# Telling the other engines that TensorE is done: a drain of its pipe, or the counters of finished products

## The chip, the cores and the metric

The kernel runs on one core of one Trainium2 chip. The metric is the device time of one execution in microseconds (us), as a median over runs. The core has five engines, each with an instruction queue of its own: TensorE (PE in the profile, its weight loads PEld), VectorE (DVE), ScalarE (ACT), GpSimd (POOL) and SyncE (SP), which here issues almost all transfers. Engines wait for each other on semaphores, counters that an instruction raises when it is done.

## The reference

One transformer block for 512 tokens of width 1024, then a second one with routed experts, all in float32.

```python
h = rms_norm(x, norm_pre[i])
(aq, ak, av, az, dq, dk, dv, db, da, dz, gate_att, gate_dn) = split_cols(h @ w_in[i])
...
o_att = gqa_attention(q, k, v).transpose(0, 2, 1, 3).reshape(B, S, ATT_W)
y_att = (o_att * jax.nn.silu(az)) @ w_br_att[i]
qkv = jax.nn.silu(short_conv(jnp.concatenate([dq, dk, dv], axis=-1), conv_w[i]))
...
o_dn = bidir_gated_deltanet(qd, kd, vd, g, beta).astype(x.dtype)
y_dn = (rms_norm(o_dn...) * jax.nn.silu(dz)) @ w_br_dn[i]
mix = (jax.nn.sigmoid(gate_att) * y_att + jax.nn.sigmoid(gate_dn) * y_dn) @ w_out[i]
x = x + rms_norm(mix, norm_post[i])
x = x + rms_norm(jax.nn.sigmoid(x @ w_ple_gate[i]) * (p[i] @ w_ple_proj[i]), ple_norm[i])
```

The second block modulates a normed x by columns computed from a condition vector (`w_ada_2`), mixes tokens by a gated linear attention in both directions and by pooling with four windows, projects with `w_out_2`, and then sends each token through two of 32 experts.

## The kernel before

The whole program is written out by hand, one instruction stream for each engine, with explicit semaphores. TensorE's stream sets the order of the work:

- Projections of the first block. Weights come in blocks of 1 MB (128 partitions, 8 chunks, 256 columns) in a fixed order, `weight_order`, into four slots, later two, then four again. SyncE's `stream_to` issues the load of block n into a slot as soon as the block that was in that slot before (`before[n]`) is used. `slot(key)` on TensorE waits for the load.
- Most projections are done two blocks at a time by `seven(u, ...)`, a scheme with seven half products instead of eight; there are 21 of these (u = 0 to 20), each some 112 matmuls of 256 columns. VectorE, ScalarE and GpSimd prepare sums of weights (`part_ready`, GpSimd line 2337) and of inputs (`term_ready`), and add up the results. The other projections are `feature_tile` and `token_tile`.
- `ada_rows` multiplies the condition by two blocks of `w_ada_2`. It is called 12 times, spread over the attention and the delta rule.
- Every product goes into one of eight PSUM banks, four of a ring called v (read by VectorE) and four of a ring called s (read by ScalarE mostly). `bank(r)` on TensorE takes the next bank of ring r and waits on `free_v` or `free_s`, and the last matmul of a product raises `full_v` or `full_s`. `jobs[r]` counts the products of a ring.
- Stage by stage the memory is used again for other things. At the end of stages 1 to 6 every engine raises `phase` by one, and whoever writes to the memory of the next stage waits until four engines have.

The stages in time, read from the lines of the instructions: projections for attention to 112 us, condition rows and turning q and k to 150, attention with gates to 262, four `seven` to 362 (stage 1 ends there), 24 tiles of the short convolution with the inverses prepared by VectorE to 571 (stage 2), eight steps of the delta rule to 689 (stage 3), output side of the first block and the start of the second to 986 (stage 4), projections, decay and pooling of the second to 1124 (stage 5), linear attention to 1176, `w_out_2` to 1250 (stage 6), routing, and from about 1284 to the end the experts, whose weights are streamed.

Three helpers of TensorE's stream and four single places tell the others that TensorE has read something for the last time. All do it by a drain: an instruction that waits until everything before it has left the array, and then raises a semaphore. `used` raises `w_used` once for each weight block, `leave_stage` and `phase` raise `phase`. The single places are one that raises `phase` at line 1460 (stage 4), one for each of four pooling products (line 1494, `pool_used`), one after the linear attention (line 1581, `gla_used`) and one at line 1638 (stage 6). One more stands in the loop over the experts (`wout_used`). In all there are 86 drains at line 1042, 4 at line 1045, and 4, 1, 1 and 1 at the single places: 97 ahead of the experts.

Of the kernel before, what the change touches and what calls it, by code (L numbers as in the profile page):

```python
# [14 lines left out]
P = 128  # L15
# [248 lines left out]
def build(nc, a, out, dumps):  # L264
    ctx = ExitStack()
    with ctx:
# [289 lines left out]
        def scratch(name, *shape):  # L556
# [11 lines left out]
        names = """chain_v chain_s chain_p phase full_v free_v full_s free_s w_used ld_const ld_vecs ld_rope  # L568
# [7 lines left out]
            lexp_ready ld_out half_win win_used wout_used ld_gs yb_ready hidT_ready sil_ready hid_ready out_ready picked_ready icol_ready rows_saved gla_used first_ready  # L576
            table_ready index_ready xg_k0 xg_k1 xe_ready st_y0 st_y1
            turns_ready sil_used pool_used zeroed dbp_ready mask_turned mask_kept last_ready""".split()
# [231 lines left out]

        block = ctx.enter_context(nc.Block())

        @block.sync
        def _(sp):
            issued = [0]

            def load(dst, src, name):
                sp.dma_start(dst, src).then_inc(s[name], 16)

            def stream_to(key):  # L820

                while True:
                    n = issued[0]
                    k, src, _, _ = weights[n]
                    if before[n] >= 0:
                        sp.wait_ge(s["w_used"], before[n] + 1)
                    sp.dma_start(slot_view(n), src).then_inc(s["ld_w", slot_of[n]], 16)
                    issued[0] += 1
                    if k == key:
                        return  # L830

            def load_win(n, x, part=0, parts=1):
                k = n % RING
                c = slice(part * KC // parts, (part + 1) * KC // parts)
                sp.dma_start(win[2 * k + x][:, c, :], win_src[n, x][:, c, :]).then_inc(s["ld_win", k], 16)

            def load_win_halves(n):
                k = n % RING
                for h, signal in ((0, s["half_win"]), (1, s["ld_win", k])):
                    c = slice(h * KC // 2, (h + 1) * KC // 2)  # L840
                    for x in range(2):
                        sp.dma_start(win[2 * k + x][:, c, :], win_src[n, x][:, c, :]).then_inc(signal, 16)

            def load_wout(n, x):
                k = n % RING
                sp.dma_start(wout[2 * k + x], wout_src[n, x]).then_inc(s["ld_wout", k], 16)

            def load_wout_early(x, c):
                sp.dma_start(wout_early[x, c], wout_src[RING, x][:, c, :]).then_inc(s["ld_pm", 0], 16)

            def save(t):
                sp.wait_ge(s["x3_ready"], t + 1)
                sp.dma_start(xn_dram[t * P:(t + 1) * P, :], x3n[:, t, :]).then_inc(s["ld_tile", t], 16)
                sp.dma_start(x3_dram[t * P:(t + 1) * P, :], x3[:, t, :]).then_inc(s["ld_tile", t], 16)

            def third_pair(t):
                sp.wait_ge(s["ld_tile", t], 48)
                sp.wait_ge(s["half_ready"], 2 * NT + NTC + t + 1)
                for x in range(2):
                    load_win(2, x, t, NT)  # L860

            for k in range(4):
                sp.dma_start(xr[:, 2 * k:2 * k + 2, :], a["x_t"][:, 2 * k:2 * k + 2, :]).then_inc(s["ld_tile", k], 16)
            stream_to(("qkv", 1))
            sp.wait_ge(s["ld_const"], 16)
            load(const[:, C_HEAD:], a["c_masks"][:, C_HEAD:], "ld_const")
            load(rope, a["c_rope"], "ld_rope")
            load(qkn[:, 0, :], a["q_norm"].partition_broadcast(P), "ld_rope")
            load(qkn[:, 1, :], a["k_norm"].partition_broadcast(P), "ld_rope")
            load(gpar[:, 0, :], a["a_log"].rearrange("a d h -> a (d h)").partition_broadcast(P), "ld_res")  # L870
            load(gpar[:, 1, :], a["dt_bias"].rearrange("a d h -> a (d h)").partition_broadcast(P), "ld_res")
            stream_to(("qkv", 3))
            sp.wait_ge(s["zeroed"], 2)
            load(y_dram[0:2 * SEQ, :].rearrange("(p r) (h n) -> p (r h) n", p=P, h=2),
                 arow.rearrange("p a n -> p (a n)").unsqueeze(1).broadcast_to([P, 16, 2 * WC]), "rows_saved")
            stream_to(("dz", 1))

            sp.wait_ge(s["phase"], 4 * 3)
            stream_to(("gd", 1))
            for t in range(NTC):  # L880
                load(ctxt[:, t, :], a["ctx_2"][0, t * P:(t + 1) * P, :], "ld_ctx")
            load(mixT.rearrange("p c n -> p (c n)"), mix_dram.rearrange("(p n) -> p n", p=P), "mix_kept")
            load(rowv, a["norm_post"].partition_broadcast(P), "ld_res")
            load(rowv2, a["ple_norm"].partition_broadcast(P), "ld_res")
            stream_to(("gd", 3))
            load(pinT, a["p_t"], "ld_p")
            stream_to(("brd", 3))
            for t in range(NT):
                load(x1[:, t, :], a["x"][0, t * P:(t + 1) * P, :], "ld_res")
            load(wa2, a["w_a2"].rearrange("p (c n) -> p c n", n=32), "ld_p")  # L890
            stream_to(("vp2", 1))

            sp.wait_ge(s["phase"], 4 * 4)
            load(bdec, a["b_decay_2"].rearrange("a d k -> a (d k)").partition_broadcast(P), "ld_small")
            sp.dma_start(gs_dram[0, :].rearrange("(c p) -> p c", p=P), gain[:, 16:24],
                         allow_slow_non_contiguous=True).then_inc(s["ld_gs"], 16)
            sp.dma_start(gs_dram[1, :].rearrange("(c p) -> p c", p=P), mod[:, 24:32, 0],
                         allow_slow_non_contiguous=True).then_inc(s["ld_gs"], 16)
            load(wpool, a["w_pool_2"][0].rearrange("g c d -> c g d"), "ld_small")
            for g in range(2):  # L900
                sp.dma_start(pm[:, g, :, :], a["c_pool"][:, g, :, :]).then_inc(s["ld_pm", g], 16)
            sp.wait_ge(s["zeroed"], 3)
            for q in range(4):
                for d in range(2):
                    load(wdec[32 * q + RANK * d:32 * q + RANK * (d + 1), d * 256:(d + 1) * 256],
                         a["w_decay_2"][0, d], "ld_small")
            stream_to(("qp2", 1))
            for g in range(2, 4):

                sp.wait_ge(s["pool_used"], g - 1)  # L910
                sp.dma_start(pm[:, g % 2, :, :], a["c_pool"][:, g, :, :]).then_inc(s["ld_pm", g % 2], 16)
            stream_to(("wo2", 1))
            sp.wait_ge(s["ld_gs"], 32)
            load(gsp[:, :, :], gs_dram.rearrange("a (p c) -> p a c", p=P), "ld_gs")
            load(wrt[:, :, 0:4], a["w_router_group_2"][0].rearrange("(c p) n -> p c n", p=P), "ld_wrt")
            load(wrt[:, :, 4:36], a["w_router_expert_2"][0].rearrange("(c p) n -> p c n", p=P), "ld_wrt")
            sp.wait_ge(s["kst_ready"], NT + NTC)
            load(wo23[0], wo23_src[0], "ld_small")

            sp.wait_ge(s["sprev_ready"], 1)  # L920
            load(wo23[1], wo23_src[1], "ld_small")

            sp.wait_ge(s["gla_used"], 1)
            for x in range(2):
                load_win(0, x)
            load_wout(2, 0)
            for t in range(NT - 1):
                save(t)
                third_pair(t)

            sp.wait_ge(s["w_used"], len(weights))
            load_win(1, 0)
            sp.wait_ge(s["phase"], 4 * 6)
            for x in range(2):
                load_wout(0, x)
            save(NT - 1)
            load(xn_dram[SEQ:, :].rearrange("o (p n) -> (o p) n", p=KC), zero[0:KC, :], "rows_saved")
            load_win(1, 1)
            for x in range(2):
                load_wout(1, x)  # L940

            sp.wait_ge(s["lg_ready"], 1)
            for k in range(2):
                sp.wait_ge(s[f"xg_k{k}"], 16)
            third_pair(NT - 1)
            for k in range(2):
                sp.wait_ge(s[f"st_y{k}"], 16)
            for x, c in wout_early:
                load_wout_early(x, c)
# [6 lines left out]
            with sp.Fori(0, rounds) as r:  # L956
# [25 lines left out]
                with sp.If(r + 1 < rounds):  # L982
                    for x, c in wout_early:
                        load_wout_early(x, c)
# [2347 lines left out]
```

## Time and profile before

| | |
|---|---|
| device time, median of 3 runs | 1535.87 us (1535.25 to 1537.34) |
| span of the profiled execution, first to last instruction | 1531.2 us |
| what lies around the span, against the median | 4.7 us |
| TensorE busy (matmuls) | 1414.3 us, 92% |
| VectorE / GpSimd / ScalarE busy | 721.2 / 420.5 / 383.3 us |
| moved by DMA | 236.51 MB |

The profiled execution's own time is not listed beside its span, so the span and the 4.7 us around it, taken against the median, stand for it. A matmul's end in the profile is modelled. Starts are recorded, so distances from start to start are what to read. "issue" as the reason of idle time means that the profile shows no wait that was fulfilled just then. Drains don't count as busy, but they can be looked up by their line.

### The profile page before, as it was taken

Reading aid. Unit: us, or ns where it says so; the run is one execution under the profiler, and the core shown is the slowest. Engines: PE = TensorE matmul, PEld = TensorE weight load, DVE = VectorE, ACT = ScalarE, POOL = GpSimd, SP = SyncE. Lnnn points to the kernel's source line nnn. Section 1 sums busy time; section 2 is a strip of 40 time slices with the busy share of each in tenths; the row PEclk is TensorE's granted clock in tenths of the full one; section 3 lists DMA queues with packets and bytes.
Section 4 is the critical chain, followed back from the end, with each engine's and each line's share of the span. In section 5 each row is a group of like instructions: output and inputs, shape, how many; then the busy total and the mean of one; then the engine's idle time right before and its main releaser. Section 6 shows DMA issues by size and latency. Waiting matters only on the chain. (4 is left out here: it accounts for less than half of the span.)

```text
span 1531.2 us, 22283 instructions
## 1 busy us (share of the span) xinstructions
PE 1414.3 (92%) x8580; PEld 959.5 (63%) x8580; DVE 721.2 (47%) x1280; ACT 383.3 (25%) x777; POOL 420.5 (27%) x316
## 2 busy tenths in 40 slices
PE   7998998999999999999999999999988979987886
PEld 5864444886454447877888868878757864332322
DVE  5251435223438987778624252731364454432325
ACT  2223445202343234332110032511251011000002
POOL 3420002630003617563555435044000003111110
PEclk9999999999999999999999999999999989999999
DMA  7227110122111212414332311241033379999996
GB/s 309 86 107 270 63 57 27 55 83 110 56 56 55 83 56 112 158 68 159 130 129 94 138 55 56 64 119 56 9 134 121 132 276 355 415 419 420 422 417 246
DMA packets 48151, 236.51 MB, mean 154 GB/s; under 512 B 12103, under 2 KB 13391, under 8 KB 27056
## 3 DMA queue, kind: packets, MB, share of 16 engines
q1 hardware_dynamic: 42432, 224.48, 37.8%
q0 software_dynamic: 5040, 8.27, 1.5%
q10 hardware_dynamic: 576, 2.36, 0.4%
q8 instruction: 69, 1.13, 0.3%
q14 instruction: 34, 0.28, 0.1%
HBM read 223.66 MB, written 21.51 MB: 160 GB/s over the span
## 5 line engine op out<-in xcount | busy, mean ns | idle before, releaser
L1092 PE MATMUL psv<-arena 128*128 128x256 f32 x1648 | 361.8, 380 | 2.9 <-issue 2.9
L1092 PEld LDWEIGHTS psv<-arena 128*128 128x128 f32 x1648 | 312.7, 190 | 47.7 <-issue 6.0
L2554 DVE TENSOR_TENSOR arena<-arena,psv 128x512 f32<-128x512 f32 (+1 forms) x99 | 68.6, 693 | 299.4 <-PE psv L1092 297.3
L1054 PE MATMUL psv<-arena,wslot 128*128 128x512 f32 x384 | 170.8, 598 | 0.5 <-issue 0.5
L1688 PE MATMUL pss<-arena 128*64 128x512 f32 x432 | 125.4, 641 | 15.8 <-DMA arena<-w_expert_in 14.6
L1054 PEld LDWEIGHTS psv<-arena,wslot 128*128 128x128 f32 x384 | 71.2, 190 | 84.0 <-issue 83.7
L1827 ACT ACTIVATE arena<-pss 128x512 f32<-128x512 f32 (+2 forms) x125 | 72.1, 577 | 152.7 <-PE pss L1054 73.5
L1054 PE MATMUL pss<-arena 128*128 128x512 f32 (+1 forms) x224 | 92.7, 566 | 6.8 <-ACTq L232 4.6
L2774 DVE SCALAR_TENSOR_TENSOR arena<-psv,ccols,arena 128x510 f32<-128x510 f32 (+1 forms) x96 | 71.9, 749 | 52.9 <-ACT arena L2007 49.6
L1092 PE MATMUL psv<-arena,wslot 128*128 128x256 f32 x384 | 86.9, 381 | 3.9 <-issue 1.9
L1688 PEld LDWEIGHTS pss<-arena 128*64 128x64 f32 x432 | 38.9, 147 | 70.4 <-issue 70.3
L1092 PEld LDWEIGHTS psv<-arena,wslot 128*128 128x128 f32 x384 | 72.4, 190 | 16.0 <-issue 5.4
L2337 POOL TENSOR_TENSOR arena<-wslot 128x1024 f32<-128x1024 f32 x11 | 25.8, 2349 | 205.6 <-PE pss L1225 114.8
L1092 PE MATMUL psv<-wslot,arena 128*128 128x256 f32 x320 | 76.8, 397 | 5.8 <-ACT arena L1886 3.5
L1092 PEld LDWEIGHTS psv<-wslot,arena 128*128 128x128 f32 x320 | 63.1, 199 | 17.3 <-ACT arena L1886 4.7
L1054 PEld LDWEIGHTS pss<-arena 128*128 128x128 f32 x224 | 41.5, 190 | 49.8 <-issue 40.7
L3236 DVE TENSOR_TENSOR arena<-pss,arena 128x256 f32<-128x256 f32 x16 | 6.8, 424 | 138.6 <-ACTq L232 138.6
L2355 POOL TENSOR_TENSOR arena<-arena 128x1024 f32<-128x1024 f32 x20 | 49.1, 2454 | 81.7 <-DVE arena L2647 36.4
L2551 DVE TENSOR_TENSOR arena<-arena 128x512 f32<-128x512 f32 (+2 forms) x64 | 51.7, 807 | 22.2 <-ACT arena L1963 11.3
L1707 PE MATMUL psv<-arena 128*64 128x512 f32 x248 | 58.5, 598 | 3.5 <-ACTq L232 2.0
L2681 DVE TENSOR_REDUCE small<-pss 128x1 f32<-128x512 f32 x32 | 22.1, 692 | 81.8 <-PE pss L1225 81.1
L2224 ACT ACTIVATE arena<-pss 128x256 f32<-128x256 f32 x16 | 6.1, 383 | 193.4 <-PE pss L1688 193.4
(397 smaller groups left out, 2079.0 us busy)
## 6 DMA issues: line engine op xcount, KB each, us to landing
wslot<-w_blocks SPq DMA_DIRECT2D x56, 1024.0 KB, 5.2
arena<-w_blocks SPq DMA_DIRECT2D x31, 1024.0 KB, 6.9
arena<-w_expert_out SPq DMA_DIRECT2D x31, 1024.0 KB, 25.4
arena<-w_expert_in SPq DMA_DIRECT2D x28, 1024.0 KB, 27.2
arena<-w_expert_in SPq DMA_DIRECT2D x28, 512.0 KB, 13.1
arena<-w_expert_in SPq DMA_DIRECT2D x6, 2048.0 KB, 19.8
y_dram<-arow SPq DMA_DIRECT2D x1, 4096.0 KB
arena<-c_pool SPq DMA_DIRECT2D x4, 1024.0 KB, 9.2
```

Source lines behind the costliest of these rows:

```text
L1054: m = mm(o, l, r, start=(n == 0), stop=(n == len(pairs) - 1))
L1092: m = mm(o[:, j * HALF_T:(j + 1) * HALF_T], l[:, c, j * P:(j + 1) * P], r[:, c, :], start=new and j == 0 and c == 0, stop=j == 1 and c == ...
L1688: m = mm(o[x * CAP:(x + 1) * CAP, :], xe[:, k, c, x * CAP:(x + 1) * CAP], win[2 * w + x][:, c, :], start=(c == 0), stop=(c == KC - 1))
L1707: m = mm(o[x * CAP:(x + 1) * CAP, :], hidT[:, k, c, x * CAP:(x + 1) * CAP], wout_home(n, x, c)[:, c0:c0 + 512], start=(c == 0), stop=(c == 1))
L1827: L.did(A(dst, src, func, **kw), s[sig] if sig else None, [s["free_s"]])
L2337: L.did(TT(part[0], a21, a22, ALU.add), s["part_ready"])
L2355: L.did(TT(term[n], lo, hi, ALU.subtract), s["term_ready"])
L2551: L.did(V.tensor_tensor(o, x, y, ALU.mult), *sig)
L2554: L.did(V.tensor_tensor(o, x, y, ALU.add), *sig)
L2681: L.did(V.tensor_reduce(c, pss[:, score_job[i] % 4, :], AXX, ALU.max))
L2774: L.did(V.scalar_tensor_tensor(o[:, lo:hi], b[:, lo + m:hi + m], tap(j, k), o[:, lo:hi], ALU.mult, ALU.add), s["conv_ready"] if k == 4 els ...
L3236: L.did(V.tensor_tensor(hid[:, k, :], pss[:, (s0 + job) % 4, DE:2 * DE], sil[:, k, :], ALU.mult), s["hid_ready"], [s["free_s"], s["sil_use ...
```

## The change

TensorE issues no drain ahead of the experts any more. While its program is written, it notes for each weight block, each pooling product and each stage how many products of the two rings had been issued by then. The other engines wait until `full_v` or `full_s` has reached that number. For this, SyncE's program is written out after TensorE's instead of before it, with no other edit in it. The semaphores `w_used`, `pool_used` and `gla_used` are gone. `phase` is raised by three engines only, so where an engine waited for `phase` alone it now waits for `phase`, `full_v` and `full_s` (`await_stage`). TensorE itself waits for `phase` once, at stage 5, as before. No matmul, transfer or operation of the other engines changes, and the drain in the experts' loop stays.

```diff
+        products_by = {}
+        stage_products = {}
+
+        def await_stage(eng, n):
+            eng.wait_ge(s["phase"], 3 * n)
+            for r, many in stage_products[n].items():
+                eng.wait_ge(s["full_" + r], many)
...
-            def used(n=1):
-                for _ in range(n):
-                    pe.drain().then_inc(s["w_used"], 1)
-
-            def leave_stage():
-                pe.drain().then_inc(s["phase"], 1)
-
-            def phase(n):
-                leave_stage()
-                pe.wait_ge(s["phase"], 4 * n)
+            def used(r, *keys):
+                for key in keys:
+                    products_by["block", at_key[key]] = r, jobs[r]
+
+            def leave_stage(n):
+                stage_products[n] = dict(jobs)
...
-                used(2)
+                used("v", *[(SEVEN[u][0], SEVEN[u][1] + j) for j in range(2)])
...
-                used(2)
+                used("s", ("ada", ada[0]), ("ada", ada[0] + 1))
...
-                        used()
+                        used("v", dqkv)
...
-                    pe.drain().then_inc(s["pool_used"], 1)
+                    products_by["pool", g] = jobs["v"]
...
-            phase(5)
+            leave_stage(5)
+            pe.wait_ge(s["phase"], 3 * 5)
...
-            pe.drain().then_inc(s["gla_used"], 1)
+            products_by["attention", 0] = jobs["s"]
...
 # SyncE, in stream_to
-                        sp.wait_ge(s["w_used"], before[n] + 1)
+                        r, many = products_by["block", before[n]]
+                        sp.wait_ge(s["full_" + r], many)
...
-            sp.wait_ge(s["phase"], 4 * 3)
+            await_stage(sp, 3)
...
-                sp.wait_ge(s["pool_used"], g - 1)
+                sp.wait_ge(s["full_v"], products_by["pool", g - 2])
...
-            sp.wait_ge(s["gla_used"], 1)
+            sp.wait_ge(s["full_s"], products_by["attention", 0])
...
 # ScalarE, VectorE and GpSimd, in phase(n)
-                act.wait_ge(s["phase"], 4 * n)
+                await_stage(act, n)
```

## Rows read from the trace of the kernel before

**Rows 1.** The page: busy time of two engines, and TensorE's granted clock in 40 slices.

```profile
PE 1414.3 (92%) x8580; PEld 959.5 (63%) x8580; DVE 721.2 (47%) x1280; ACT 383.3 (25%) x777; POOL 420.5 (27%) x316
...
PEclk9999999999999999999999999999999989999999
```

**Rows 2.** The drains by line: duration ns min/median/max, first and last start us.

```profile
L1042 PEldq DRAIN  x86: 13/1550/8012, 41.0 to 1237.0; - x86
```

**Rows 3.** TensorE's timeline, `seven`: start us, us, instructions; two boundaries with a stop, one without.

```profile
73.80 7.07 PE L1092 MATMUL psv<-arena 128*128 128x256 f32 x32
80.71 3.62 PE L1092 MATMUL psv<-wslot,arena 128*128 128x256 f32 x16
```

```profile
69.31 0.59 PE L1092 MATMUL psv<-arena 128*128 128x256 f32 x2
70.28 0.45 PE L1092 MATMUL psv<-wslot,arena 128*128 128x256 f32 x1 [0.38 <-issue]
```

```profile
794.82 0.59 PE L1092 MATMUL psv<-arena 128*128 128x256 f32 x2
795.90 0.45 PE L1092 MATMUL psv<-arena,wslot 128*128 128x256 f32 x1 [0.48 <-issue]
```

**Rows 4.** TensorE's timeline, convolution: one boundary without a stop, one with.

```profile
384.15 1.02 PE L1054 MATMUL psv<-arena,wslot 128*128 128x512 f32 x2
385.10 0.28 PE L1362 MATMUL pss<-const,arena 128*64 128x1 f32 x4
```

```profile
392.70 1.02 PE L1054 MATMUL psv<-arena,wslot 128*128 128x512 f32 x2
393.98 0.31 PE L1362 MATMUL pss<-const,arena 128*64 128x1 f32 x5 [0.26 <-issue]
```

**Rows 5.** TensorE's timeline: `ada_rows` in the delta rule and the next product.

```profile
595.71 0.61 PE L1155 MATMUL pss<-wslot,csilu 128*32 128x256 f32 x8
596.72 0.25 PE L1279 MATMUL pss<-arena 32*32 32x32 f32 x5 [0.41 <-issue]
```

**Rows 6.** TensorE's waits for the rest of the chip: total us, times, longest us.

```profile
PE psv L1092 <- issue: 5.6, 14, 0.5
```

**Rows 7.** Busy by stretch: length, five engines' us (instructions), clock, DMA share, GB/s.

```profile
466.90:564.10 97.20, 95.42 (x417) 44.83 (x416) 89.80 (x128) 28.86 (x48) 42.78 (x68) 1.00 0.18 65
568.20:571.60 3.40, 1.59 (x45) 1.27 (x37) 1.21 (x2) 1.87 (x4) 0.00 (x0) 1.00 0.02 5
571.60:575.00 3.40, 3.17 (x14) 1.60 (x16) 1.20 (x2) 0.70 (x2) 2.20 (x3) 0.50 0.00 0
587.00:606.00 19.00, 18.34 (x326) 14.29 (x322) 16.63 (x39) 6.32 (x18) 10.76 (x10) 1.00 0.32 117
894.80:914.30 19.50, 18.87 (x72) 10.77 (x72) 16.45 (x21) 9.80 (x16) 0.00 (x0) 1.00 0.29 108
972.00:990.00 18.00, 17.74 (x99) 15.72 (x97) 15.16 (x17) 9.40 (x21) 0.00 (x0) 1.00 0.03 10
1284.00:1496.00 212.00, 183.78 (x832) 69.12 (x830) 65.15 (x157) 11.71 (x30) 39.65 (x69) 0.94 1.01 417
```

**Rows 8.** Waits of VectorE from 466 to 571 us, then of all from 563 to 571.5.

```profile
DVE arena L2774 <- ACT arena L2007: 1.2, 2, 0.8
```

```profile
PE pss L1138 <- ACT arena L2039: 1.5, 1, 1.5
...
PE pss L1279 <- issue: 1.0, 1, 1.0
```

**Rows 9.** SyncE's timeline from 104 to 144 us, and TensorE's waits from 111 to 142.

```profile
133.75 2.54 SPq L827 DMA_DIRECT2D wslot<-w_blocks  x2
```

```profile
PE pss L1155 <- issue: 2.7, 3, 2.2
```

**Rows 10.** TensorE's timeline after the linear attention, and at the end of stage 5.

```profile
1178.99 0.96 PE L1604 MATMUL pss<-arena,const 128*32 128x512 f32 x4 [2.23 <-ACT arena L2200]
```

```profile
1124.37 0.49 PE L1510 MATMUL pss<-const,arena 128*128 128x128 f32 x2 [0.90 <-POOLq L2451]
```

More of the change, by code:

```diff
@@ L566, in build @@
         pss = ctx.enter_context(nc.psum_tensor("pss", [P, 4, 512], F32))
[L568 removed]
+        names = """chain_v chain_s chain_p phase full_v free_v full_s free_s ld_const ld_vecs ld_rope
             ld_res ld_p ld_ctx ld_small ld_rowf ld_wrt silu_z xn_ready hT_ready
@@ L809, in eliminate @@
             L.did(V.tensor_tensor(o, o, t, ALU.add))
-        block = ctx.enter_context(nc.Block())
[L813 to L825, printed above, removed]
-                        sp.wait_ge(s["w_used"], before[n] + 1)
[L827 to L876, printed above, removed]
-            sp.wait_ge(s["phase"], 4 * 3)
[L879 to L908, printed above, removed]
-                sp.wait_ge(s["pool_used"], g - 1)
[L911 to L921, printed above, removed]
-            sp.wait_ge(s["gla_used"], 1)
[L924 to L949, printed above, removed]
-            load(rowf, a["final_norm_g_2"].rearrange("(a n) -> a n", a=1).partition_broadcast(P), "ld_rowf")
-            sp.wait_ge(s["lexp_ready"], 4)
-            sp.wait_ge(s["turns_ready"], 2)
-            load_wout(2, 1)
-            rounds = rounds_of(sp)
-            with sp.Fori(0, rounds) as r:
-                def next_win(n):
-                    for part in range(pieces[n]):
-                        sp.wait_ge(s["win_used"], r * FREED + (freed_by[n - RING] - pieces[n] + 1 + part))
-                        if n == NP - 1:
-                            load_win_halves(n)
-                        else:
-                            for x in range(2):
-                                load_win(n, x, part, pieces[n])
-                def next_wout(n, used):
-                    sp.wait_ge(s["wout_used"], r * NP + used)
-                    for x in range(2):
-                        if n != RING or (x, 0) not in wout_early:
-                            load_wout(n, x)
-                next_win(RING)
-                for n in range(RING + 1, NP - 2):
-                    next_win(n)
-                    next_wout(n - 1, n - RING)
-                next_wout(NP - 3, NP - 2 - RING)
-                next_win(NP - 2)
-                next_wout(NP - 2, NP - 1 - RING)
-                next_win(NP - 1)
-                next_wout(NP - 1, NP - RING)
-                with sp.If(r + 1 < rounds):
-                    for x, c in wout_early:
-                        load_wout_early(x, c)
-                    for k in range(RING):
-                        used = max(n for n in range(NP) if n % RING == k) + 1
-                        sp.wait_ge(s["win_used"], r * FREED + freed_by[used - 1])
-                        for part in range(pieces[k]):
-                            for x in range(2):
-                                load_win(k, x, part, pieces[k])
-                        sp.wait_ge(s["wout_used"], r * NP + used)
-                        for x in range(2):
-                            sp.dma_start(wout[2 * k + x], wout_src[k, x]).then_inc(s["ld_wout", k], 16)
-            sp.wait_ge(s["win_used"], last_of(sp) * 4 + 3)
-            def x3_again(t):
-                sp.dma_start(x3[:, t, :], x3_dram[t * P:(t + 1) * P, :]).then_inc(s["ld_tile", t], 16)
-            for t in READ[:2]:
-                x3_again(t)
-            for k in range(2):
-                sp.wait_ge(s[f"st_y{k}"], rounds * (NP // 2 * 16) + 16 * (1 - k))
-            for t in READ:
-                if t in READ[2:]:
-                    x3_again(t)
-                for k in range(2):
-                    sp.dma_start(ygat[:, k, t, :], y_dram[k * SEQ + t * P:k * SEQ + (t + 1) * P, :])\
-                        .then_inc(s["ld_tile", t], 16)
-            for n, t in enumerate(END):
-                sp.wait_ge(s["out_ready"], n + 1)
-                sp.dma_start(out[0, t * P:(t + 1) * P, :], x3[:, t, :]).then_inc(s["ld_out"], 16)
-            for name, ap in dumps:
-                sp.dma_start(name, ap).then_inc(s["ld_out"], 16)
-            sp.wait_ge(s["ld_out"], 16 * (NT + len(dumps)))
@@ L1348, in _ @@
                 if j < 24:
+                    dqkv = ("dqkv", (j // 2 + 4) % 8 if j < 16 else j // 2)
                     if j % 2 == 0:
-                        w = slot(("dqkv", (j // 2 + 4) % 8 if j < 16 else j // 2))
+                        w = slot(dqkv)
                     assert jobs["v"] == conv_job(j), (jobs["v"], conv_job(j))
@@ L1459, in _ @@
                 token_tile("s", wv1, t, hcT)
-            pe.drain().then_inc(s["phase"], 1)
+            leave_stage(4)
             for t in range(NT):
@@ L1637, in _ @@
                 if t == NT - 1:
-                    pe.drain().then_inc(s["phase"], 1)
+                    leave_stage(6)
                 logits(t - 1)
@@ L2078, in _ @@
             hold_first(7, held_b)
-            act.wait_ge(s["phase"], 4 * 3)
+            await_stage(act, 3)
             corner_of(7, gates, ACT.Silu)
@@ L2277, in phase @@
                 pool.sem_inc(s["phase"])
-                pool.wait_ge(s["phase"], 4 * n)
+                await_stage(pool, n)
             def rows(n):
@@ L2451, in _ @@
             pool.sem_inc(s["phase"])
-            pool.wait_ge(s["phase"], 4 * 6)
+            await_stage(pool, 6)
             L.did(nc.gpsimd.memset(xg, 0.0))
@@ L2538, in phase @@
                 dve.sem_inc(s["phase"])
-                dve.wait_ge(s["phase"], 4 * n)
+                await_stage(dve, n)
             def squares(v, dst, j):
```

196 lines of the change are left out of this document (186 added, 10 removed).

## Prediction

> **What bounds the kernel now.** I read the page first. TensorE is busy for 92% of the span, VectorE for 47%, and the granted clock is at its upper level, 2.4 GHz, nearly everywhere [rows 1]. So up to the experts TensorE sets the pace, and time taken from it there counts unless something else is late by then. The experts differ: from 1284 to 1496 us the DMA share is 1.01 at 417 GB/s [rows 7]. That stretch gets no shorter, but it starts as soon as TensorE and routing let it, so a gain before it arrives whole at the end.
>
 I call a place where one or more drains follow each other a stop. There are 62: 21 after `seven` (two drains each, three at the end of stage 1), 12 after `ada_rows` (two each), 12 in the convolution, and 17 others (16 with one drain, one with two).
>
> **What a stop costs.** Read from start to start. Without a stop, 32 matmuls of 256 columns begin at 73.80 and the next product at 80.71: 0.216 us each, also across the boundary. With a stop, the last matmul begins at 69.31 + 0.59 - 0.38 = 69.52 and the next product at 70.28: 0.76, which is 0.54 too much. Where the next product has one more wait ahead, it is 795.90 - 795.04 = 0.86, 0.65 too much [rows 3]. TensorE's own waits show the same: 14 idle times of line 1092 with no releaser, 5.6 us in total, 0.40 each [rows 6], counted from modelled ends. In the convolution the same boundary stands once without and once with a stop: 385.10 - 384.58 = 0.52 against 393.98 - 393.13 = 0.85, so 0.33 [rows 4]. After `ada_rows`, 596.72 - 595.94 = 0.78 [rows 5]. Less 0.22 that is 0.56, and as a product on another part of the array costs 0.1 even without a stop (0.52 against 0.43 for a matmul of 512 columns) [rows 4], I take 0.50.
>
> The gross sum: after `seven` 12 x 0.54 + 8 x 0.65 + 0.4 (the first, into the narrow product at 94 us) = 12.1. `ada_rows` 12 x 0.50 = 6.0. Convolution 12 x 0.33 = 4.0. Of the 17 others two are worth nothing: after the linear attention TensorE waits 2.23 us for ScalarE anyway, and at the end of stage 5 0.90 us for the others' `phase` [rows 10], both released by work that begins at the same last matmul. The 15 others lie between 0.27 and 0.54, together 5.7. Gross 27.8 us.
>
> **What is taken back.** After a stop is gone, TensorE arrives earlier, and where its next input comes from a chain that doesn't start at the stop, it waits instead.
> - Convolution, second half. From 466.9 to 564.1 us VectorE is busy for 89.8 of 97.2 us in 128 instructions [rows 7], which leaves 0.06 between two, and it waits 1.2 us for ScalarE [rows 8]. It is full. At the end TensorE waits for what comes from it, 1.0 and 1.5 us [rows 8]. The first six stops come through, the six from 482 on only lengthen those waits: -2.0.
> - Condition rows, 96 to 142 us. A block's load takes some 6 us from release. The one issued at 133.75 is needed at once, and `ada_rows` waits 2.2 of the 2.7 us in [rows 9] for it (no releaser is shown). The same happens once earlier, by 0.3 us. The stops between release and need, two each time, turn into waiting: -2.0. One more, at 141.6, loses half: -0.3.
> - Delta rule, first steps. From 587 to 606 VectorE is busy for 16.6 of 19.0 us in 39 instructions [rows 7], full again, so of the stops at 596 and 612 about 0.25 remains: -0.75. Later VectorE has idle time, and these stops count. The stop at the end of stage 3 comes ahead of waits for VectorE's work of that stage: -0.4.
> - 894.8 to 914.3 and 972 to 990: VectorE busy 16.5 of 19.5 and 15.2 of 18.0 us [rows 7], on chains that begin with the end of the `seven` before. Of two stops each, 0.4 remains in the first pair, nothing in the second: -0.6 and -1.1. At 741 us turns wait for their banks: -0.4.
> - Pooling: the third matrix lands just when it is needed, its load released by the first product: -0.7, and -0.35 after the last product.
>
> Together -8.5, leaving 19.3.
>
> **What is added.** `await_stage` has up to two more waits at each of some 19 places. A further wait costs about 0.86 - 0.76 = 0.10 us [rows 3]. Perhaps five lie on the path: -0.5 (between 0 and -1.9). Queued behind each are the first operations of the next stage on that engine, and TensorE waits for them only at the starts of stages 3 and 4. Behind SyncE's waits stand all later loads. These come no later, since a counter rises with the very matmul that the drain waited for, and the second block of a pair is released 0.1 sooner. Now the clock. TensorE was busy for only 1.59 us from 568.2 to 571.6, and from 571.6 to 575.0 the granted clock is 0.50, that is 1.2 GHz [rows 7]. With 2 us more waiting just ahead of it, one more such stretch is possible. It costs half of its 3.4 us, 1.7. I take half of that as the likely value: -0.8 (between 0 and -1.7).
>
> **The sum.** 27.8 - 8.5 - 0.5 - 0.8 = 18.0 us. The profiled execution has a span of 1531.2 us, and against the median 4.7 us lie around it, which the change doesn't touch. 1513.2 + 4.7 = 1517.9.
>
> **The rivals.**
> - A, everything comes through. VectorE's full stretches might contain slack that the short gaps hide. For it speaks that TensorE shows no wait inside the convolution. Against it are the waits at the end. Gain 24 to 28 us, time 1510.
> - B, others pace more than I see. Where TensorE's waits are just covered, 0.5 us less brings one out. For it: VectorE and ScalarE wait on each other in attention and delta rule, and every step there is a loop through TensorE. Then mostly the stops between one `seven` and the next count, 12 to 14 of them with 0.6 us each, and half of the convolution's: gain 7 to 12, time 1526.
> - C, no change: the drains would stand where TensorE waits anyway. Some do [rows 10]. But [rows 3] show none of the other waits at the restart, so this needs most stops to be overtaken later. Time 1534 to 1537.
> - D, slower, through the clock. Longer single rests could drop the clock to 1.2 GHz in stretches that are full now, each costing about 1.7 us. To eat 18 us and 3 more takes 12 such stretches before the experts, where the row of slices shows nearly none now [rows 1]. Time 1539 or more. The Trainium skill (TensorE: Matmul & The Clock Gate, "HAM oscillation — how this bites in real kernels") describes kernels that fall back to the lower clock again and again after waits. The trace agrees that a wait can do it, at 571.6 us, but this change shortens far more rests than it lengthens.
> - E, the change doesn't do what it says: if the counters' waits let loads go later than the drains did, the sevens would wait for weights. The loads are needed some 20 us after their release there, so even 1 us would not show. It has no time of its own and counts with C.
>
> **Chances.** Forecast (gain 13 to 23 us) 0.60, A 0.10, B (with anything from 3 to 13 us) 0.20, C with E 0.05, D 0.05. About 0.2%, 3 us, is what a measurement tells from no change. Faster 0.90, same 0.05, slower 0.05. The forecast's own range is 1513 to 1523. To leave out no more than 2 in 10 the range takes in A's middle and most of B: 1510 to 1526. The likeliest time is 1518.
>
> **What the profile after would show.** No drain ahead of the experts, and boundaries of `seven` at 0.22 us from start to start. The convolution's boundaries all at 0.52. TensorE's wait at the end of the convolution 2 us longer (if not, A). The wait ahead of `ada_rows` near 137 us 1 us longer. The shift of the start of stages, against before: 3 us at 150, 6 at 362, 8 at 571, 10 to 11 at 689, 14 to 15 at 986, 18 at 1250, and from there on constant. If the shift grows by less within attention or the delta rule, that is B. If it shrinks anywhere, it is the clock or a load. The forecast is wrong most easily in the stretches that I called free: a wait just covered now can cost any single stop its gain.

## The result

The changed kernel takes 1511.13 us, median of 4 runs (1509.53 to 1513.9), beside 1535.56 us (1530.15 to 1537.34, 4 runs) of the kernel before on the same chip: ratio 0.9855, 95% interval [0.9835, 0.9876], so a gain of 19 to 25 us by the interval. On two other chips it came out at 1512.42 us (one run, before 1534.17) and at 1513.18 us (6 runs, 1509.6 to 1518.41, before 1531.54; ratio 0.9884 [0.9862, 0.9906], a gain of 14 to 21 us). Both intervals hold 19 to 21 us, so I take some 20 as the change's worth, and the forecast's 18.0 lies a little under it. The median itself, 1511.13, lies 6.8 us under the likeliest time of 1518 and outside the forecast's own range (1513 to 1523). It is inside the stated range of 1510 to 1526 because that took in rival A's middle.

The profiled execution took 1509.53 us by its own time with a span of 1507.5, so 2.0 us lie around the span, not the 4.7 that the prediction took from a median that was not this execution's.

The page of the changed kernel, against [rows 1]: the same 8580 matmuls, 8.3 us less of them busy by the modelled ends, and a span shorter by 23.7 us. Nothing stands on line 1042 or in place of it. The only drain left is the one in the experts' loop.

```profile
span 1507.5 us, 22203 instructions
...
PE 1406.0 (93%) x8580; PEld 959.9 (64%) x8580; DVE 720.6 (48%) x1280; ACT 383.6 (25%) x777; POOL 421.2 (28%) x316
...
PEclk9999999999999999999999999999999989999999
```

TensorE's timeline of the changed kernel, at the places of [rows 3] (the first five rows), at two boundaries of the convolution (the next four: the one that has a stop in [rows 4], and the next, which had none), at [rows 5] (two), pooling, and [rows 10] (the last two):

```profile
68.98 3.62 PE L895 MATMUL psv<-wslot,arena 128*128 128x256 f32 x16
72.43 7.07 PE L895 MATMUL psv<-arena 128*128 128x256 f32 x32
79.34 4.91 PE L895 MATMUL psv<-wslot,arena 128*128 128x256 f32 x22
...
777.73 6.21 PE L895 MATMUL psv<-arena 128*128 128x256 f32 x28
783.77 3.62 PE L895 MATMUL psv<-arena,wslot 128*128 128x256 f32 x16
...
379.49 6.60 PE L857 MATMUL psv<-arena,wslot 128*128 128x512 f32 x15
386.02 0.63 PE L1166 MATMUL pss<-const,arena 128*64 128x1 f32 x16
...
387.51 7.13 PE L857 MATMUL psv<-arena,wslot 128*128 128x512 f32 x16
394.58 0.57 PE L1166 MATMUL pss<-const,arena 128*64 128x1 f32 x14
...
585.16 1.93 PE L958 MATMUL pss<-wslot,csilu 128*32 128x256 f32 x32
587.03 0.69 PE L1082 MATMUL pss<-arena 32*32 32x32 f32 x32
...
1093.01 3.70 PE L857 MATMUL psv<-arena 128*128 128x512 f32 x8 [0.65 <-DMA arena<-c_pool]
...
1103.82 1.16 PE L1315 MATMUL pss<-const,arena 128*128 128x128 f32 x8 [0.91 <-ACTq L1873]
...
1158.46 1.60 PE L1409 MATMUL pss<-arena,const 128*32 128x512 f32 x8 [2.24 <-ACT arena L2211]
```

The 16 matmuls at 68.98 take 72.43 - 68.98 = 3.45, 0.216 each. In the kernel before the same 16, right behind a stop, took 73.80 - 70.28 = 3.52 [rows 3]. So besides the late first matmul the second one was late too, by 0.07. In the convolution both boundaries now stand at 0.52 to 0.53 (386.02 - 385.50, 394.58 - 394.06). The waits at the end of stage 5 and after the linear attention are as long as before, 0.91 and 2.24 us, so the stops ahead of them were indeed worth nothing.

The waits and stretches of the changed kernel where the prediction saw gains taken back (columns as in [rows 6] and [rows 7]):

```profile
PE pss L1082 <- issue: 3.1, 1, 3.1
PE pss L958 <- issue: 2.4, 2, 1.5
...
PE pss L857 <- DMA wslot<-w_blocks: 0.9, 1, 0.9
```

```profile
457.70:553.00 95.30, 95.30 (x420) 44.74 (x420) 88.23 (x127) 28.76 (x47) 42.87 (x68) 1.00 0.19 67
554.80:558.10 3.30, 1.05 (x40) 1.04 (x42) 3.01 (x4) 0.32 (x1) 1.00 (x1) 1.00 0.63 263
558.10:564.90 6.80, 6.14 (x66) 3.83 (x60) 2.05 (x3) 3.01 (x7) 1.32 (x3) 0.50 0.01 2
```

TensorE's wait at the convolution's end grew from 1.0 to 3.1 us, the forecast's 2.0. A stretch at 1.2 GHz follows, as feared, earlier and twice as long (558.1 to 564.9, against 571.6 to 575.0 [rows 7]).

**The shift.** The best single view of this change is the start of the same matmul in two traces, as a difference. The second column is against the trace shown ahead of the prediction. The fourth is that of another execution of the kernel before (below, e8), and the last takes that one as the base.

| start before, us | after | forecast | before again | after against before again |
|---|---|---|---|---|
| 112.8 | 2.19 | | -0.55 | 2.7 |
| 150.4 | 3.42 | 3 | 0.62 | 2.8 |
| 361.9 | 6.41 | 6 | 0.62 | 5.8 |
| 568.4 | 8.39 | 8 | 0.60 | 7.8 |
| 689.1 | 10.19 | 10 to 11 | 0.92 | 9.3 |
| 986.9 | 15.89 | 14 to 15 | 0.83 | 15.1 |
| 1002 | 17.28 | | 2.51 | 14.8 |
| 1122.9 | 20.55 | | 2.57 | 18.0 |
| 1250.9 | 21.63 | 18 | 2.61 | 19.0 |
| 1278 | 21.49 | 18 | 2.12 | 19.4 |

The same difference can be followed stop by stop. From the last matmul ahead of a stop to the first behind it, the shift jumps by the stop's price: 0.54 or 0.65 after most `seven`, 0.33 in the convolution (0.43 once), 0.47 after ten of the twelve `ada_rows` and 0.33 after the other two, and 0.00 at the two stops that were to be worth nothing. Over the 62 stops these jumps add up to 26.6 us, and with the second matmul, which is late behind most `seven`, to 27.8. What is not there at 1250.9 was taken back between the stops. 0.6 us of the last column stood already at 40 us, ahead of the first stop, so the stops bring 18.5 us there, and 9.3 were taken back.

### The profile page after: what moved, and what is told of

The parts are those of the page before. It is cut to its first block and busy times, and to the rows that moved or that the text cites. A ratio compares the mean times of both kernels' runs of the same rounds, so it can differ in the third digit from the quotient of the medians.

```text
span 1507.5 us, 22203 instructions
## 1 busy us (share of the span) xinstructions
PE 1406.0 (93%) x8580; PEld 959.9 (64%) x8580; DVE 720.6 (48%) x1280; ACT 383.6 (25%) x777; POOL 421.2 (28%) x316
```

## The experiments

Ten kernels ran. Seven of them put drains back into the changed kernel or fill its rests, three are repetitions. A bare drain is `pe.drain()` without a semaphore, which nobody waits for.

**e1, e2: all drains back, and one for each stop.** In `used`, `leave_stage` and at the single places:

```diff
             def used(r, *keys):
                 for key in keys:
                     products_by["block", at_key[key]] = r, jobs[r]
+                for _ in range(len(keys)):     # e2: range(1)
+                    pe.drain()
...
                 stage_products[n] = dict(jobs)
+                pe.drain()
```

> The changed kernel with all 97 drains back at their places ahead of the experts, but bare: they raise nothing, and the others still wait for the counters. Theory (the restart of TensorE after a stop is the whole price): the gain is gone, a span of 1531 us give or take 2, 0.98 to 0.99 of nothing won against before. Rival (the gain comes from what stands in the drains' place: earlier releases of weights, SyncE's program written later, one semaphore less to raise): most of the gain stays, a span of 1508 to 1515.

> As the kernel with all drains bare, but with one drain at each of the 62 stops instead of up to three (only the 86 at the weight blocks are thinned out, to one per place). Theory (a stop costs a restart, and each further drain only about 0.12 us, from 0.013 us of its own and the step to it): 34 x 0.12 = 4 us less than with all 97, some of it taken back, so a span of 1527 to 1529. Rival (each drain costs the same, 23.7 us over 97 drains is 0.24 each): 34 x 0.24 = 8 us less, 1523.

e1: 1532.41 us (10 runs), ratio 0.9985 [0.9961, 1.0009]. e2: 1528.12 us (10 runs), 0.9963 [0.9939, 0.9987]. So the counters, the waits of `await_stage` and the new order of SyncE's program together can't be told from nothing (between 6 us gained and 1 lost by the interval), and the drains are the price. One stop of e2, at the end of stage 1, kept two drains, so it has 63. Up to 1123 us e1 grows its shift by 2.6 us from 112.8, where the changed kernel grows it by 18.4, and the other execution of before by 3.1 with no edit at all.

TensorE's timeline of e1 and then of e2 at the first boundary of [rows 3], and behind each the idle times of line 898 from the waits:

```profile
70.56 3.69 PE L898 MATMUL psv<-wslot,arena 128*128 128x256 f32 x16 [0.29 <-issue]
74.09 7.07 PE L898 MATMUL psv<-arena 128*128 128x256 f32 x32
```

```profile
PE psv L898 <- issue: 4.6, 14, 0.4
```

```profile
68.76 3.69 PE L898 MATMUL psv<-wslot,arena 128*128 128x256 f32 x16 [0.22 <-issue]
72.29 1.03 PE L898 MATMUL psv<-arena 128*128 128x256 f32 x4
```

```profile
PE psv L898 <- issue: 3.5, 14, 0.3
```

Beside the 5.6 us of [rows 6] this is a price list. The 14 idle times are 0.40 each with two drains that raise a semaphore, 0.33 with two bare ones, 0.25 with one, and none without. The first drain carries the cost. The second adds 0.08, and that they raise adds 0.07 for the pair. The lower price of bare drains (0.07 at each of the 21 `seven`, less at the others) is about what e1 gains: 1.1 us on e8 from 112.8 to 1123, without the stretch near 998 us that e1 has and e8 has not. So nothing is left for the counters. My 0.12 for a further drain was too high. e2 does lie 4.3 us ahead of e1 at 987, as expected, but 1.9 of that stood already at 112.8, and 1.4 at 20 us, where e2 had a stretch of 3.4 us at 1.2 GHz and e1 one of 6.8. Between 112.8 and 987 it is 2.4 us.

**e3, e4: the two parts.** e3 has the bare drains only after the 21 `seven`, e4 only at the 41 other stops and one more behind the seventh `seven`, where stage 1 ends.

```diff
+                if keys[0] in SEVEN:           # e4: not in SEVEN, and the other places
+                    for _ in range(len(keys)):
+                        pe.drain()
```

> The changed kernel with bare drains after the 21 sevens only, two each. Theory with the sizes read from both traces (0.61 or 0.72 for a stop between one seven and the next, as the second matmul after a stop is late as well, and three or four of the 21 covered by VectorE's chains): 10 to 12 us slower than the changed kernel, a span of 1518 to 1520. By the prices of the forecast, 0.54 and 0.65 and less what was called taken back, it would be 9 to 10 us. Rival (stops are worth the same everywhere, 23.7/62 = 0.38): 8 us.

> The complement: bare drains at the 41 other stops and none after the sevens. Theory: convolution 2 us (six of its twelve), condition rows, gates and delta rule 4 to 5, stages and pooling 1, last projection 1, together 8 to 10 us slower than the changed kernel, a span of 1516 to 1518. If the costs of the two parts add up, this one and the one with the sevens' stops together lose what the one with all drains loses. If they fall short of it, stops of one kind cover those of the other.

e3: 1523.68 us (6 runs), ratio 0.9924 [0.9895, 0.9952]. e4: 1519.97 us (4 runs), 0.9893 [0.9851, 0.9936]. In the traces, from 112.8 to 1123, e3's shift grows by 10.7 and e4's by 13.7 us where the changed kernel's grows by 18.4. The drains of 18 `seven` cost 7.7 us there (0.43 each), those of the others 4.7. Together that is 12.4. All of them together, in e1, cost 18.4 - 2.6 = 15.8, of which 1.7 is the stretch at 998 us (below): 14.1. Parts that cost less one by one than together fit the covered waits of the prediction: where one set of stops is gone, TensorE waits in a few places for others, and a stop of the other set ahead of such a wait is free. That was not followed wait by wait. By the medians the parts gain 10.0 us (e3) and 13.7 us (e4) on before, the whole 18 to 24.

Both parts cost less in the traces than I expected: 10 to 12 us for all 21 `seven`, which at 0.43 each would be 9, and 8 to 10 for the others. The spans of the two traces, 1522.3 and 1520.9, lie above the expected ones all the same. The linear attention ran at 1.2 GHz for 17 us in e3 and 20 in e4, and 3.4 in the changed kernel.

**e5, e6: the two halves of the convolution.** One bare drain after each of the 12 first tiles, or of the 12 last. That is twice as many as before had.

```diff
                     feature_tile("v", w, j % 2, hT)
                     if j % 2:
                         used("v", dqkv)
+                    if 0 <= j < 12:            # e6: 12 <= j < 24
+                        pe.drain()
```

> The changed kernel with a bare drain after each of the first 12 tiles of the short convolution, where VectorE has 2.5 to 7 us of idle time per tile pair. Theory (a stop counts where VectorE isn't full): read in the trace, the start of the convolution's tile 12 comes 12 x 0.33 = 4.0 us later than in the changed kernel, and the start of the delta rule 3.5 to 4 us later. Rival (stops count or don't count in both halves alike): the delta rule starts as much later here as with the stops in the second half.

> The same 12 bare drains after the last 12 tiles, where VectorE is busy for 89.8 of 97.2 us. Theory: TensorE's wait at the end of the convolution, 3.3 us in the changed kernel, shrinks to nothing first, so the delta rule starts only 0 to 1 us later, although the last tile comes 4.0 us later. Rival: the delta rule starts 3.5 to 4 us later.

This is the clearest of the experiments. From 369 us to 587, the first steps of the delta rule, the changed kernel's shift grows by 2.1 us, in e7 and e10 as well. With 12 drains in the first half it shrinks by 1.7, so 3.8 are lost, 0.32 for each drain. With 12 in the second half it still grows by 1.0, so 1.1 are lost for the same number. (Read at 575, where the trace of before runs at 1.2 GHz, it is 4.0 and 0.7.) At 987 us the losses are the same 3.8 and 1.1. The waits of the two at the convolution's end, e5 and then e6:

```profile
PE pss L1082 <- issue: 3.1, 1, 3.1
PE pss L941 <- ACT arena L2052: 1.1, 1, 1.1
```

```profile
PE pss L941 <- ACT arena L2052: 1.5, 1, 1.5
```

In e5 TensorE comes to the end 4 us late, and still waits 3.1 us there. So VectorE came just as late, and its work is paced by TensorE's first tiles. VectorE's own starts show it: at 550 us, counted from 369 us, they are 3.8 us later in e5 than in the changed kernel, and not later in e6. In e6 the wait of line 1082 is gone: the drains ate it. VectorE is full in the second half and sets the end, as step "Convolution, second half" of the prediction had it.

**e7, e8: the same kernels again.** The changed kernel and the kernel before, unedited, on another chip.

> The changed kernel once more, for its trace: does the stretch at half clock at 998 us of the kernel before, which is gone after the change and gave 1.4 us, stay away, and does the one of 6.8 us at the end of the convolution come again? If the stretches are set by where the chip's own time grid falls, they come and go between runs, and the start of each stage moves by 1 to 2 us between two traces of the same kernel. If they are set by the kernel's waits, both traces agree within 0.3 us at every stage.

> The kernel before once more, for its trace. If the half clock at 998 us belongs to the kernel's waits it is there again and the stages start where they did within 0.3 us. If it is chance, then it may be gone, and with it 1.4 us of the 23.7 that the two first traces differ by, so that the change itself is worth about 22.

1512.42 and 1530.64 us. e7's shifts agree with those of the changed kernel's first trace within 0.5 us up to 1123. At 1159 it is behind by 2.3 us: 18.20. So of my two answers neither fits everywhere: the kernel repeats itself up to the linear attention, and there the stretches came at other places. The stretch of 6.8 us at the end of the convolution came again (at 558.0, in e10 at 557.8). e8 shows how much of the table is chance: 1.2 us at 137, where its load came sooner, and 1.7 at 998, where the first trace of before had a stretch at 1.2 GHz and e8 had none. Neither had the changed kernel, so its step from 15.89 to 17.28 there is not the change's. Nor had e8 the stretch that begins at 571.6 in the first trace of before, though the work and the rests ahead of that place are the same in both. First e8, then the first trace:

```profile
566.50:570.90 4.40, 2.62 (x64) 2.10 (x62) 2.25 (x3) 2.43 (x6) 0.50 (x1) 1.00 0.23 91
570.90:574.40 3.50, 2.19 (x18) 1.14 (x18) 2.04 (x3) 0.86 (x3) 2.28 (x2) 1.00 0.00 0
```

```profile
567.10:571.50 4.40, 2.62 (x64) 2.10 (x61) 2.25 (x3) 2.43 (x6) 0.50 (x1) 1.00 0.22 91
```

The stretch cost the first trace nothing that lasted: e8's shift is 0.60 at 571 and 0.52 at 587. The stretches of e7 in the linear attention:

```profile
1117.80:1121.20 3.40, 3.24 (x36) 2.69 (x40) 1.72 (x6) 0.18 (x1) 0.00 (x0) 0.50 0.69 207
1124.60:1128.00 3.40, 3.40 (x26) 2.95 (x26) 1.96 (x5) 0.01 (x1) 0.00 (x0) 0.50 0.00 0
...
1162.10:1165.50 3.40, 3.40 (x10) 2.67 (x9) 2.79 (x1) 0.51 (x1) 0.00 (x0) 0.51 1.02 439
```

In e1 they were 27.3 us long in all, one of them 17.1 us with TensorE busy for 16.7 of it, and took its shift from 2.35 at 1123 to -6.7 at 1186. That accounts for e1's profiled execution being its slowest, 1539.78 us, where the fastest of its ten took 1528.39:

```profile
1142.50:1145.90 3.40, 3.40 (x34) 2.99 (x35) 1.47 (x4) 0.60 (x1) 0.00 (x0) 0.50 0.00 0
1156.20:1173.30 17.10, 16.73 (x130) 15.48 (x131) 2.57 (x10) 0.20 (x1) 0.00 (x0) 0.50 0.18 63
1183.50:1190.30 6.80, 5.65 (x17) 3.30 (x18) 4.37 (x3) 2.06 (x4) 0.00 (x0) 0.50 0.96 373
```

**e9, e10: TensorE's rests filled, beside the changed kernel once more.** If the rests around the linear attention bring the lower clock on, matmuls of constants in their place should keep it up.

```diff
+            def keep_busy(o, n):
+                for _ in range(n):
+                    mm(o[:, 0:P], ident, ident, start=True, stop=True)
...
             leave_stage(5)
+            taken = bank("s")                  # the first product takes it over
+            keep_busy(taken, 4)
...
+            taken = bank("v")
+            keep_busy(taken, 12)
             L.need(s["kst_ready"], NT + NTC)
...
+            o = bank("s")
+            keep_busy(o, 12)
             L.need(s["sq2_ready"], H2)
-            o = bank("s")
```

> The changed kernel, plus 28 matmuls of 128x128 constants that TensorE issues while it would wait: 4 at the end of stage 5, 12 ahead of the linear attention's state products, 12 after the linear attention. They write into the bank that the next real product takes and overwrites, so they add no result. Theory 1 (the changed kernel's scatter comes from stretches at half clock that TensorE's rests between 1117 and 1186 us bring on, up to 17 us long in the drain kernels, 3.4 to 10 us in the changed one): with the rests filled, no stretch at half clock between 1117 and 1180 us; the shift against before at 1159 keeps the 20.5 us that it had at 1123; median 1 to 4 us under the changed kernel's (1507 to 1510) and the runs closer together. Rival (a matmul that runs into the end of a wait delays the product behind it, and the clock falls anyway): stretches at half clock stay, and the time is 0 to 1.5 us above the changed kernel's (1511 to 1513).

> The changed kernel unchanged, beside the one with filled rests on the same chip: 1511 (1508 to 1515), 22 to 25 us under before, with stretches at half clock somewhere between 1117 and 1180 us, 3 to 14 us in all. If the changed kernel's first runs were lucky, it comes out at 1514 or more.

e9: 1514.07 us (6 runs, 1511.49 to 1518.36), e10: 1513.18 (6 runs, 1509.6 to 1518.41). No gain, and a scatter of 6.9 us against 8.8. My theory fell, at least in this form, and the rival's outcome came. e10's gain of 18.4 us also misses the 22 to 25 that I expected. The rests were filled, as e9's timeline shows (12 matmuls of the program stand as 24 in it), but 10.2 us at 1.2 GHz came all the same, at 1135.7 instead of 1117.6:

```profile
1115.21 2.84 PE L1306 MATMUL psv<-const 128*128 128x128 f32 x24
1117.98 0.68 PE L1361 MATMUL psv<-arena 64*64 64x128 f32 x16
...
1141.27 3.75 PE L1386 MATMUL pss<-arena 128*128 128x128 f32 x16 [0.38 <-issue]
...
1147.34 2.05 PE L1386 MATMUL pss<-arena 128*128 128x128 f32 x16
```

```profile
1135.70:1145.90 10.20, 9.82 (x83) 8.92 (x82) 2.96 (x11) 0.20 (x1) 0.00 (x0) 0.50 0.30 104
```

The last group of 12 overran its rest: from the last real matmul ahead of it to the next behind it pass 3.08 us, 2.51 in the changed kernel, so e9 loses 0.6 us by its own filling. e10's timeline at the product of 1117.98: it starts right behind the rest, and at the lower clock.

```profile
1118.01 1.15 PE L1353 MATMUL psv<-arena 64*64 64x128 f32 x16 [2.41 <-DVE arena L2562]
1119.08 2.08 PE L1364 MATMUL psv<-arena 64*128 64x128 f32 x16
```

That looks as if the long rest set where the stretch begins. But the changed kernel's first trace has the same rest of 2.4 us and no stretch before 1158.9, so by itself it does not bring one on, and without it one comes. Between 1117 and 1135 TensorE still rests six times in e9, for 0.18 to 0.65 us between short products, which the filling left alone. Whether those do it was not tried, and what brings the lower clock on here stays open.

## Why the prediction was right

The outcome lies on the side and in the range that were forecast, and the mechanism is the one named: the restarts cost what was read off, and about a third of it is taken back. The range is in part luck, as said above: the first comparison gained 24.4 us for a forecast of 13 to 23, and the repetitions, 21.8 and 18.4, are inside. Point by point, by the prediction's own steps:

- **"What a stop costs".** The boundaries lost what was read off: the convolution's 0.33 (e5: 3.8 us for 12), `ada_rows` 0.46 for a forecast 0.50 (587.03 less 586.71, the last start before it, is 0.32 where 0.78 stood [rows 5]). For `seven`, 0.54 and 0.65 were mis-sized. They measured only the first matmul behind the stop, and the second is late by another 0.07. Over the 21 that is 1.3 us, since behind a few there is less of it. Whoever reads a restart from start to start has to read one matmul further. The measured sum, 26.6 and 1.2, is the forecast's 27.8 by luck: the other prices came out 1.2 lower. That the price is one of "restarting the sequencer" no run shows; they show what a drain costs, not which part of the engine takes the time.
- **Two stops worth nothing.** Right, by the two waits of unchanged length.
- **"Convolution, second half", -2.0.** Right: the wait grew by 2.1 us, and e6 shows that 12 drains there cost 1.1.
- **"Condition rows", -2.0 and -0.3.** Right in kind. Against the other execution of before the shift grows by 0.1 from 112.8 to 150, so the stops there bring nothing. The waits became 2.4 us at line 958 and 0.9 for a weight block at 118. In the trace that I forecast from, the wait near 137 us lasted 2.2 us and in e8 0.8, by chance, so after the change it was 1.5 and not 1 us longer than in that trace.
- **"Delta rule", -0.75 and -0.4.** From 571 to 689 the shift grows by 1.7 us, and by 1.4 against e8. I expected 2 to 3. So a little more was covered than I took. The stop at the end of stage 3 brings nothing: 0.32 at the stop, and 0.32 less by the next `seven`.
- **894 to 914 and 972 to 990, -0.6 and -1.1.** The first pair is right: from 894.4 us, ahead of its first stop, to 937.9, ahead of the next `seven`'s, the shift grows from 14.18 to 14.51, where 0.4 was to remain. The second is mis-sized: from 964.5 to 998.1 it grows from 14.83 to 15.59, so 0.8 of the 1.0 us of its two stops remains, where nothing was to. VectorE being busy for 15.2 of 18.0 us did not make it full. The turns at 741 us took back 0.5, for 0.4.
- **Pooling, -0.7 and -0.35.** The third matrix now makes TensorE wait 0.65 us, and the shift falls by 0.8 there, as forecast. The other is 0.1: between the last two products stand 2.98 us for 2.86.
- **"What is added", -0.5 for the waits of `await_stage`.** Not seen. e1 has all of these waits, and its stages start no later than the kernel's before. It is nothing, or less than 0.5.
- **The clock, -0.8.** The stretch at the convolution's end came, 6.8 us for 3.4. From 565 to 580 the shift falls from 11.26 to 8.75, by 2.5 us. The wait grew by 2.1, and the stop at 571, 0.4 gross, lies in between, and the wait after it got shorter (1.5 to 0.7), so net some 0.8 is left for the longer stretch and whatever else lies there. All three traces of the changed kernel have the stretch, so they can't tell what it cost. Rival D's sentence that the trace agrees that a wait can bring the lower clock on does not stand: e8 has the same rests and keeps 2.4 GHz. What the clock did elsewhere is larger than this term and goes both ways, in kernels with the change and without.
- **The experts.** The sum let the gain arrive whole. From 1278 to the end the shift changes by +2.3 in the first trace, +2.1 in e7 and +1.7 in e10, and by +0.6 in e8 and +0.1 in e1 and e4. But it changes by -2.7 in e5 and -1.6 in e6, whose code from the convolution on is the changed kernel's. So that stretch varies by itself, by more than the change could be giving there, and whether it gives 1 to 2 us is open.
- **"The sum".** By the shift at 1250.9 it was 21.6 us against the trace that I had, and 19.0 against e8. e7 and e10 stand at 19.3 and 19.2 against the first, 16.7 and 16.6 against e8. Of the figures against e8, 0.6 to 0.7 stood ahead of the first stop, so the stops bring 18.5, 16.1 and 15.9 us, and 9.3 to 11.9 of their 27.8 are not there. The forecast had 9.8 for this (its own items of what is taken back add up to 8.6, not 8.5). So its 18.0 is right in size for what the stops bring. What the first comparison has beyond it is within the chance that the repetitions show: 1.7 us at 998, about 2 in the linear attention, 1.2 at 137, 2 in the experts. The time around the span was mis-sized: it is 2.0 us (2.1 in e8), not 4.7. In the executions recorded with both figures it is 2.0 to 3.7, so the profiled execution of before took some 1533 to 1535 us by this estimate, and 1 to 2.7 of what I took for time around the span were scatter between executions.
- **Rivals.** A (everything comes through, 24 to 28 us) has the first median on its side, but is out by its mechanism, since e6 and the grown waits show gain taken back. B asked for a gain of 7 to 12 us and is out by every comparison. C and E are out, and so is D for the total, though e1 shows that the clock can take 9 us from one execution. C fell by the jumps at the stops and E by the loads: no `seven` waits for a weight block.

## What to carry to other kernels

In this kernel a drain on TensorE that raises a semaphore cost by what stands behind it: 0.54 to 0.65 us for two of them before the next product of 256 columns, 0.33 for one before the convolution's narrow ones, nothing ahead of a wait. Where the last matmul of a product raises a semaphore anyway, that counter said the same here at no cost that the runs show, and a generator of kernels can note the count while it writes the program.

Forecast such a sum gross, then go through the stretches in which another engine has no gap left, and take back what lies ahead of the next wait for it. Here that was a third of the gross sum or a little more, and the halves of the convolution (3.8 us lost against 1.1 for the same 12 drains) show how sharp the border is.

Take two executions of the kernel before, not one, before a shift of 1 to 2 us is explained: the same kernel gave 1.2 us at one load and 1.7 at one stretch of the clock.

## What the runs showed of the hardware

- Of a drain's price, the first one carries the most: 0.25 us idle by the modelled ends for one, 0.08 for a second one behind it, 0.07 for the pair when both raise a semaphore. The matmul after the next is late by 0.07 too. Ahead of waits of 0.90 and 2.23 us [rows 10] a drain cost nothing.
- Two executions of the kernel before, with TensorE busy for the same 2.62 of 4.40 us and the same rest of 1.54 us in it, went on differently: one at 1.2 GHz for 3.4 us (571.6 to 575.0), one at 2.4 GHz.
- Through the linear attention the granted clock falls to 1.2 GHz for 3.4 to 27 us in all, in the same kernel at another place from run to run (1158.9 in the first trace of the changed kernel, 1117.8, 1124.6 and 1162.1 in e7, and nearly the same as those in e10). It did so with TensorE busy for 16.73 of 17.1 us within such a stretch, and just as well when the rests of 0.9, 2.4 and 2.2 us were filled with matmuls. The Trainium skill ("TensorE: Matmul & The Clock Gate", "HAM oscillation — how this bites in real kernels") describes a kernel that falls back again and again after waits. That it falls again and again the traces of e1 and e7 show. That the waits do it they leave open, since filling the three longest does not end it, and the changed kernel's first trace has the same rests with a single stretch.
